# Expert rows scattered with an add into one DRAM row per token, and a tail that reads that row instead of eight slots

## The reference, cut to what matters

```python
scores = sigmoid(t @ router_w)                 # 384 tokens, 64 experts
_, idx = top_k(masked, 8)                      # 8 experts of each token
gates  = normalised scores of those 8 * 2.5
hid    = silu(t @ exp_w_gate) * (t @ exp_w_up) * gates      # per expert, FF = 256
routed = sum over experts of hid @ exp_w_down               # rows of 1024
shared = (silu(t @ sh_w_gate) * (t @ sh_w_up)) @ sh_w_down
x = x + gate2 * (routed + shared)
y = rmsnorm(x, final_g)
```

## Time and profile before

| What | Value |
|---|---|
| runs | 1304.66 us median of 3, 1301.41 to 1308.70 |
| the profiled execution | 1304.72 us, its span 1302.6 us |
| busy share of the span | PE 88%, DVE 82%, ACT 61%, POOL 17% |
| TensorE clock granted | 0.94 mean, 1.00 in the expert stage |
| DMA | 328.05 MB, mean 252 GB/s |
| queue 1 (loads and stores of SP) | 294.66 MB, 64.3% of 16 engines' span |
| queue 0 (POOL's DMAs) | 29.57 MB, 6.2% |
| chain that ended last | PE 31%, DMA 28%, DVE 26%, of it DMA `raw<-in_exp_w_down_dram` 23% |
| first and last scatter issued | 627.49 and 1235.78 us |

### The profile page before, as it was taken

How to read it: one execution, slowest core, us unless ns; L and a number is a source line. 1 busy time by engine, 2 the same in 40 slices (tenths; PEclk the granted TensorE clock), 3 DMA queues, 4 the chain that set the end, 5 groups by cost and what they waited for, 6 DMA issues and landing times.

```text
span 1302.6 us, 17353 instructions
## 1 busy us (share of the span) xinstructions
PE 1151.5 (88%) x5707; PEld 945.0 (73%) x5707; DVE 1067.8 (82%) x1456; ACT 797.4 (61%) x1018; POOL 215.9 (17%) x144
## 2 busy tenths in 40 slices
PE   3899999789989999698999999999999999999800
PEld 1599999654558967677887877788888888887600
DVE  2769999999976734566988889899999899998648
ACT  5553333567766422336877777788878778887601
POOL 1000000300000000011521212224435123142100
PEclk9799999889999979589999999999999999999955
DMA  8563456325436153428999999999999999999396
GB/s 313 170 167 97 138 161 176 117 65 162 162 117 206 65 176 119 165 93 293 376 355 343 365 340 361 345 354 357 360 341 370 348 350 368 357 357 338 140 341 244
DMA packets 142044, 328.05 MB, mean 252 GB/s; under 512 B 28053, under 2 KB 69352, under 8 KB 133159
## 3 DMA queue, kind: packets, MB, share of 16 engines
q1 hardware_dynamic: 120424, 294.66, 64.3%
q0 software_dynamic: 19264, 29.57, 6.2%
q10 hardware_dynamic: 2304, 3.15, 0.7%
HBM read 325.06 MB, written 44.19 MB: 283 GB/s over the span
## 4 chain that ended last, share of the span: by engine, by line
PE 31%; DMA 28%; DVE 26%; issue 6%; ACT 6%; SPq 2%; DVEq 0%; POOL 0%; ACTq 0%; POOLq 0%
DMA raw<-in_exp_w_down_dram 23%; PE bank L1548 9%; PE bank L1550 9%; PE bank L1549 9%; DVE lo L1434 7%; DVE lo L1439 5%; ACT hi L950 4%; DVE lo L1038 3%; DVE zb L1139 2%; DMA raw<-in_mod_w_dram 2%; SPq L595 2%; DMA slots<-sh_d 1%; DVE slots L1502 1%; DVE mx L1214 1%; DMA y_d<-ys,ixt 1%
## 5 line engine op out<-in xcount | busy, mean ns | idle before, releaser
L1434 DVE TENSOR_TENSOR lo<-raw,hi 128x2048 fp32r<-128x2048 f32 x128 | 292.5, 2286 | 5.9 <-ACT hi L943 5.9
L943 ACT ACTIVATE hi<-raw 128x2048 fp32r<-128x2048 f32 x128 | 244.2, 1909 | 4.9 <-issue 4.9
L1548 PE MATMUL bank<-hi,xgh 128*128 128x512 f32 x512 | 209.6, 409 | 10.6 <-DVE lo L1434 9.9
L1550 PE MATMUL bank<-hi,xgl 128*128 128x512 f32 x512 | 201.1, 393 | 0.0
L1549 PE MATMUL bank<-lo,xgh 128*128 128x512 f32 x512 | 199.8, 390 | 0.0
L950 ACT ACTIVATE hi<-raw 128x2048 fp32r<-128x2048 f32 x64 | 122.8, 1919 | 115.4 <-DMA raw<-in_exp_w_down_dram 115.4
L1439 DVE TENSOR_TENSOR lo<-raw,hi 128x2048 fp32r<-128x2048 f32 x64 | 146.7, 2293 | 51.0 <-ACT hi L950 50.7
L1038 DVE TENSOR_TENSOR lo<-raw,hi 128x2048 fp32r<-128x2048 f32 (+2 forms) x65 | 142.3, 2195 | 47.8 <-ACT hi L726 47.8
L726 ACT ACTIVATE hi<-raw 128x2048 fp32r<-128x2048 f32 (+2 forms) x65 | 119.0, 1834 | 33.2 <-PE bank L1550 28.0
L694 POOL DMA_INDIRECT y_d<-ys,ixt x64 | 129.3, 2021 | 50.2 <-ACT ys L981 30.5
L1139 DVE SCALAR_TENSOR_TENSOR zb<-zb,cwt 128x400 f32<-128x400 f32 x240 | 135.5, 636 | 0.6
(11 more groups left out here) (286 smaller groups left out, 2161.0 us busy)
## 6 DMA issues: line engine op xcount, KB each, us to landing
raw<-in_exp_w_gate_dram SPq DMA_DIRECT2D x128, 512.0 KB, 6.5
raw<-in_exp_w_up_dram SPq DMA_DIRECT2D x128, 512.0 KB, 10.8
raw<-in_exp_w_down_dram SPq DMA_DIRECT2D x64, 1024.0 KB, 12.2
raw<-in_mod_w_dram SPq DMA_DIRECT2D x24, 1024.0 KB, 5.3
slots<-y_d SPq DMA_DIRECT2D x6, 2048.0 KB, 15.4
raw<-in_w_in_dram SPq DMA_DIRECT2D x16, 512.0 KB, 5.4
raw<-in_w_in_dram SPq DMA_DIRECT2D x8, 1024.0 KB, 5.3
raw<-in_w_o_attn_dram SPq DMA_DIRECT2D x4, 1024.0 KB, 4.9
```

The source lines that it names most:

```text
L943: act.activation(dst, src, ACT.Copy).then_inc(ghi_done, 1)
L1434: dve.tensor_tensor(l, src, h.bitcast(F32), ALU.subtract).then_inc(glo_done, 1)
L1548: pe.matmul(out, ah, bh, start=first, stop=False)
L1550: return pe.matmul(out, al, bh, start=False, stop=last)
```

## The change

The routed rows no longer have slots. `acc_d` has one row per token and starts as the shared expert's output. Each expert's scatter adds its rows to it inside the DMA. Since two experts of one token write the same row, each scatter now waits until the one before it has landed (the first waits for the store of the shared part). The router no longer computes a rank within a token. The tail loads one 4 KB row per token; `tg`, `fgr` and `tx` have places of their own and are issued as the expert stage ends.

```diff
+        tx = sb("tx", [P, NT, D], 0)
+        tg = sb("tg", [P, 2, D], 16)
+        ta = sb("ta", [P, NT, D], 32)
+        tout = sb("tout", [P, NT, D], 44)
...
-        y_d = dram("y_d", [T * TOPK, D])
-        sh_d = dram("sh_d", [P, NT, D])
+        acc_d = dram("acc_d", [T, D])
...
-            sp.dma_start(sh_d, shy[:, :, :]).then_inc(sh_out, 16)
+            sp.dma_start(acc_d.rearrange("(t p) d -> p t d", p=P), shy[:, :, :]).then_inc(sh_out, 16)
...
+            sp.dma_start(fgr[:, :], final_g.rearrange("(a n) -> a n", a=1).partition_broadcast(P)).then_inc(fgr_in, 16)
+            sp.wait_ge(glo_done, even2)
+            sp.dma_start(tx[:, :, :], x1_d).then_inc(tx_in, 16)
+            sp.wait_ge(dlo_done, even)
+            sp.dma_start(tg[:, :, :], g2_d).then_inc(tg_in, 16)
+            sp.wait_ge(gu_filled, N)
             for u in range(2):
                 sp.wait_ge(scattered[u], sent)
...
+            for t in range(NT):
+                sp.dma_start(ta[:, t, :], acc_d[t * P:(t + 1) * P, :]).then_inc(acc_in[t], 16)
...
             def scatter(i, k):
                 j = i * UNROLL + k
-                filled = value(pool, j + 1)
+                filled, earlier = value(pool, j + 1), value(pool, uses(i, k - 1) * 16)
                 pool.wait_ge(rtab_done, 1)
                 pool.wait_ge(ys_done, filled)
-                pool.indirect_dma_start(y_d, bass.IndirectOffsetOnAxis(ap=ixt[:, k % UNROLL, 1:2], axis=0),
-                                        ys[k % 2][:, :], None,
-                                        bounds_check=TOPK * T - 1, oob_is_err=False).then_inc(scattered[k % 2], 16)
+                if from_step(j, 1):
+                    pool.wait_ge(scattered[(k - 1) % 2], earlier)
+                else:
+                    pool.wait_ge(sh_out, 16)
+                pool.indirect_dma_start(acc_d, bass.IndirectOffsetOnAxis(ap=ixt[:, k % UNROLL:k % UNROLL + 1], axis=0),
+                                        ys[k % 2][:, :], None, compute_op=ALU.add,
+                                        bounds_check=T - 1, oob_is_err=False).then_inc(scattered[k % 2], 16)
...
+            act.activation(stat[:, 63:64], stat[:, 48:49], ACT.Sqrt)
...
+                act.activation(tjunk[:, :], ta[:, t, :], ACT.Square, accum_out=stat[:, 16 + t:17 + t]).then_inc(tss_done, 1)
...
-            for t in range(NT):
-                ins = dve.tensor_tensor_scan(rrk[:, t, :], ones[:, 0:NE], rmsk[:, t, :], 0.0, ALU.mult, ALU.add)
-            link(dve, "v", ins)
-            link(dve, "v", dve.tensor_tensor(rrk[:, :, :], rrk[:, :, :], rmsk[:, :, :], ALU.subtract))
...
-                dve.tensor_scalar(ixt[:, k % UNROLL, :], p[:, 0:2], float(NO_TOKEN), None, ALU.add)
-                dve.tensor_reduce(gsl[:, k % UNROLL:k % UNROLL + 1], p[:, 2:4], AX, ALU.add).then_inc(list_done, 1)
+                dve.tensor_scalar(ixt[:, k % UNROLL:k % UNROLL + 1], p[:, 0:1], float(NO_TOKEN), None, ALU.add)
+                dve.tensor_reduce(gsl[:, k % UNROLL:k % UNROLL + 1], p[:, 1:3], AX, ALU.add).then_inc(list_done, 1)
...
+            def summed(t):
+
+                dve.wait_ge(acc_in[t], 16)
+                link(dve, "v", dve.tensor_tensor(ta[:, t, :], ta[:, t, :], tg[:, cond_of(t), :], ALU.mult))
+                dve.tensor_tensor(ta[:, t, :], ta[:, t, :], tx[:, t, :], ALU.add).then_inc(t2_done, 1)
...
+            for t in range(NT):
+                summed(t)
+                if t:
+                    normed(t - 1)
             normed(NT - 1)
```

More of the change, by code:

```diff
@@ L274, in hybrid_step @@
         hdl = [sb(f"hdl{i}", [P, FF], R + 14 + i, F32R) for i in range(2)]
[L276 to L279, removed]
+        tx = sb("tx", [P, NT, D], 0)
+        tg = sb("tg", [P, 2, D], 16)
+        ta = sb("ta", [P, NT, D], 32)
+        tout = sb("tout", [P, NT, D], 44)
+        tjunk = sb("tjunk", [P, D], A + 97)
         fgr = sb("fgr", [P, D], A + 105)
-        tjunk = sb("tjunk", [P, 512], A + 109)
-        tout = [sb(f"tout{i}", [P, D], A + 113 + 4 * i) for i in range(2)]
         sig_d = dram("sig_d", [16, P, T])
@@ L618, in _ @@
             sp.wait_ge(shy_done, 2 * NT)
-            sp.dma_start(sh_d, shy[:, :, :]).then_inc(sh_out, 16)
+            sp.dma_start(acc_d.rearrange("(t p) d -> p t d", p=P), shy[:, :, :]).then_inc(sh_out, 16)
             last = in_order(sp, step)
-            N = value(sp, last * UNROLL + UNROLL)
+            N, even = value(sp, last * UNROLL + UNROLL), value(sp, last * UNROLL + UNROLL - 1)
+            even2 = value(sp, (last * UNROLL + UNROLL - 1) * 2)
             sent = value(sp, (last * UNROLL + UNROLL) * 8)
             sp.wait_ge(rtab_done, 1)
-            sp.wait_ge(dn_filled, N)
-            sp.wait_ge(ys_done, N)
+            sp.wait_ge(x1_out, 16)
+            sp.wait_ge(sh_out, 16)
+            sp.dma_start(fgr[:, :], final_g.rearrange("(a n) -> a n", a=1).partition_broadcast(P)).then_inc(fgr_in, 16)
[4 more added lines that the diff above has]
+            sp.wait_ge(gu_filled, N)
             for u in range(2):
                 sp.wait_ge(scattered[u], sent)
[L630 to L646, removed]
+            for t in range(NT):
+                sp.dma_start(ta[:, t, :], acc_d[t * P:(t + 1) * P, :]).then_inc(acc_in[t], 16)
             for t in range(NT):
@@ L649, in _ @@
                 dst = y_prompt[0] if t == 0 else y_sample[0, (t - 1) * P:t * P, :]
-                sp.dma_start(dst, tout[t % 2][:, :]).then_inc(y_out[t % 2], 16)
-            for u in range(2):
-                sp.wait_ge(y_out[u], 16 * ((NT + 1 - u) // 2))
+                sp.dma_start(dst, tout[:, t, :]).then_inc(y_out, 16)
+            sp.wait_ge(y_out, 16 * NT)
             sp.wait_ge(cks_out, 32)
@@ L1013, in _ @@
             act.wait_ge(sh_out, 16)
-            in_order(act, step)
-            for t in range(NT):
[L1018 to L1024, removed]
+            last = in_order(act, step)
+            sent = value(act, (last * UNROLL + UNROLL) * 8)
+            act.activation(stat[:, 63:64], stat[:, 48:49], ACT.Sqrt)
+            act.wait_ge(rtab_done, 1)
+            for u in range(2):
+                act.wait_ge(scattered[u], sent)
+            for t in range(NT):
+                act.wait_ge(t2_done, t + 1)
+                if t:
+                    act.wait_ge(tss_done, t)
+                act.activation(tjunk[:, :], ta[:, t, :], ACT.Square, accum_out=stat[:, 16 + t:17 + t]).then_inc(tss_done, 1)
                 act.wait_ge(trv, t + 1)
@@ L1528, in _ @@
+            dve.wait_ge(tx_in, 16)
+            dve.wait_ge(tg_in, 16)
+            for t in range(NT):
+                summed(t)
+                if t:
+                    normed(t - 1)
             normed(NT - 1)
```

56 lines of the change are left out of this document (14 added, 42 removed).

## The result

The changed kernel takes 1339.94 us (median of 4 runs, 1337.80 to 1342.67); the kernel before, beside it on the same chip, 1304.37 (1301.41 to 1308.70). The ratio is 1.026, 95% interval [1.0234, 1.0286]: slower by 35.6 us, where 11 were forecast.

The account below looks back on a forecast made before the run. The prediction took DMA to bound most expert-stage steps, with compute close behind. From 1304.7 us, - 43.0 (tail) + 42.7 (read) + 9.8 (chain) + 1.5 (last scatters) gave 1316 us, range 1275 to 1378.

Parts of the forecast that it names:

- tail: After the last scatter's landing: loading and adding slots shrinks to three 512 KB loads, 63.6 to 20.6 us, giving back 43.0.
- read of the add: Expert stage: each adding scatter also reads its DRAM row, 2794 rows at 0.0153 us, +42.7 us.
- chain: Expert stage: each scatter waits for the one before to land, a step at least landing plus 0.3 us; +9.8 us.
- last scatters: End of the expert stage: a second row adds about 1 us to each, so the last lands +1.5 us later.
- third rival: Expert stage: a few DMA engines carry all added rows, +66 us instead of +42.7, total 1339; chance 0.12.
- second rival: Expert stage: scatter landing plus 0.3 us sets the step, 11.1 to 12.3 us; whole 1329 to 1397; chance 0.24.
- router: Router: scans and three small operations go, a copy comes; counted as nothing, at most 1.5 us of gain.

Follow-up runs that it names:

- two accumulators: Changed kernel with two DRAM accumulators, experts alternating between them, scatters adding without waiting for the one before: 1325.72 us, ratio 1.0146.
- two accumulators with plain writes: Changed kernel with two alternating DRAM accumulators and no scatter chain, scatters writing instead of adding (sum over experts left out): 1266.56 us, ratio 0.9705.
- The spread pairs: Expert token lists spread over the 128 partitions, against packed: kernel before 1286.74 us, changed kernel 1293.62, two accumulators 1267.69, two accumulators with plain writes 1248.78.
- plain writes in the chain: Changed kernel, each scatter still waiting for the one before, but writing instead of adding (sum over experts left out): 1263.55 us, ratio 0.9652.
- the chain alone: Kernel before with one wait added, each scatter waiting until the one before has landed, no adds, old tail: 1311.64 us, ratio 1.0022.

## Why the prediction was off

The span of the profiled execution went from 1302.6 to 1339.0 us. By the prediction's own terms:

| term | predicted | measured | by |
|---|---|---|---|
| tail | -43.0 | -44.5 | the windows |
| read of the add | +42.7 | +57.7 (50 to 58) | two accumulators, with add less without |
| chain | +9.8 | +12.7 (13 to 20) | the changed kernel less two accumulators (+12.3 on the kernel before) |
| last scatters | +1.5 | +12.9 | the windows |
| one row per token, the rest of the stage | 0 | -2.2 | two accumulators with plain writes less before |

They sum to +36.6, the difference of the spans to 0.2; the three terms of the stage do so by construction. The uncertainty of the read and of the chain is one and the same, the long profiled execution of two accumulators: what one loses the other gains.

**The read of the add: 7 to 15 us too small.** The step that failed is its price for a row. It had been taken from a slope of time by pairs, 0.0153 us a row, in which, as we read it now, steps that DMA sets were mixed with steps that compute sets: in the latter a row cost nothing, and the mean of both was taken for a rate of the DMA. That nothing lower than one more row would stand came true; one more row was dearer than reckoned. The third rival, a few engines carrying the added rows, had said +66 for the term, as far from the 50 to 58 on its side as the forecast on its own, and got a chance of 0.12 although the trace already spoke for it (268 GB/s a row in a stage that moves 354). Its total, 1339, is the measured time; that is luck in part, since its term was too large and it kept the 1.5 for the last scatters. The spread pairs and the counts of packets show the cause that it named. The Trainium skill (DMA: Bandwidth & Descriptors, section "The descriptor swizzle") puts, for a transfer to 128 partitions, the first 64 on eight of 16 engines; the 8.1 engines of the row's price agree with it, so do the 27.0 us with exactly 8 packets under way, and so does the effect of a permutation that was made by it. Which partition belongs to which engine no trace here shows, since the packets carry no engine's name.

**The last scatters: 11.4 us mis-sized.** The step said that a second row adds about 1 us to each, and allowed 1.5 for all. At the end, with the weight loads over, the added scatter lands after 5.2 to 6.0 us instead of 2.8 to 3.2, is issued in 1.55 us instead of 0.97, and the next waits for it. From the 58th scatter to the last one pass 39.3 us before, 40.1 with two accumulators and plain writes, 45.8 with two accumulators and adds and 49.4 in the changed kernel. So the add makes some 6 us of it and the chain 4. The mistake was to price one landing, where six follow each other. A part of it may come from loads: `fgr`, `tx` and `tg` are issued from 1281.1 to 1285.7 us, just behind the scatter of 1280.58, which took 12.56 us to land and stands in the chain. With plain writes in the chain, the scatter of 1232.36 took 7.07 us with these loads beside it; the same one with the chain alone, where nothing is loaded then, took 3.19. No run separates how much of the 12.9 that is.

**The chain: right in size on the kernel before (6 to 12 us against 9.8), some us too small with adds (13 to 20), by a step of which one part was wrong.** The gap between a landing and the next scatter is 0.87 us, not the 0.3 of two instructions of POOL in a row. The trace of before had rows for it: ACT's `ys` ended at 1201.73 and POOL's scatter began at 1202.59. Against that, landings got shorter when the issue was late, as the prediction argued from the scatter at 937.51: with the chain alone the mean is 9.27 us, where it was 9.82. The two errors cancelled.

**The second rival's sign came, but its reason did not.** (Its sums are 2 us too high: by its own terms they come to 1327 and 1395.) ACT waits for scatters in nearly all steps and steps are 11.18 us, in its range of 11.1 to 12.3. Whoever stops at the profile settles for it. Taking the chain out gives 13 to 20 us of the 68, since the wait for weights comes back with 144 us. The test that the prediction wrote down ("If ACT's wait in L980 for a scatter is tens of us and its wait for weights falls, the chain has taken over") can't tell 13 us from 68: where two limits lie 2% apart, the wait goes almost wholly to the one that ends last. The stage grew by 68.2 us, inside the 25 to 75 by which the prediction would hold itself right, though a term in it was 7 to 15 us off.

**The tail and the router** came as reckoned: 19.1 us against 20.6, and nothing. Three loads of 512 KB in place of twelve and a half MB of slots are all that it needs. `tx`, `tg` and `fgr` cost nothing ahead of it without a chain (with two accumulators and plain writes 40.1 us from the 58th scatter to the last, against 39.3 before); with the chain they may have cost a few us, as said.

## What to carry to other kernels

The total of a wait tells which limit ends last, not what it costs; that is found by taking it away, and the next limit's distance sets the gain (13 to 20 us here packed, 37.3 spread, for the same chain). Traffic that leaves an idle tail for a stage bound by DMA is paid at that stage's rate, and a scatter that adds pays for a second row. Before a packed list of rows goes into an indirect DMA, spread it over the partitions: three lines in a table of constants made the kernel before 1.4% faster, and with adds into two accumulators on top it ran at 0.9712 [0.9655, 0.9769] of its time.

## What the hardware did that was not expected

- An indirect DMA that adds costs about one more copied row of 4 KB (0.018 to 0.0207 us packed, 0.0057 spread, where compute hides a part; 0.168 us of one engine in both), and the profile's bytes don't count it.
- The partitions in which valid rows lie changed the stage by 21.5, 36.1 and 60.7 us (slots, adds in a chain, adds into two accumulators) with the same bytes. Packed, 8 packets or fewer were under way for 21.6, 52.2 and 49.2 us of it, spread for 0.8, 5.8 and 0.4.
- With spread lists and plain writes or slots, PE is busy for all of the 547.5 us, 9.6 us a step, though 11 steps of the kernel before took 9.1, and 7 of its own. The number of pairs may be part of it; it wasn't tried.
- POOL starts 0.8 to 0.9 us after a landing that it waits for.
